# Triangular inverses held as two stacked 64-blocks, in one transformer kernel on a Trainium2 core

## The reference

```
L = where(strict, einsum(kb, k) * decay, 0)
sol = triangular_solve(L, [v * beta, kb * exp(g)], unit_diagonal=True)
S = S * g_last + kd^T v_new ;  o = qd S + a_qk v_new
```

```
sa = state a_t
state = state * w_t + sa b_t^T + v_t k_t^T
y = state r_t
```

## Time and profile before

| | us |
|---|---|
| median of 3 runs (1602.46 to 1609.0) | 1608.83 |
| profiled execution, first to last instruction | 1608.8 |
| TensorE busy | 1542.6 (96%) |
| VectorE busy | 1066.1 (66%) |
| ScalarE busy | 732.4 (46%) |
| GpSimd busy | 69.8 (4%) |

### The profile page before, as it was taken

The page is one execution under the profiler, slowest core; times in us unless marked ns, Lnnn a source line. Parts: engine busy times, 40 slices in busy tenths (PEclk is TensorE's granted clock), DMA queues, the critical chain, the costliest instruction groups (busy, mean ns, idle before and its releaser), DMA issues.

```text
span 1608.8 us, 35749 instructions
## 1 busy us (share of the span) xinstructions
PE 1542.6 (96%) x15477; PEld 1482.4 (92%) x15477; DVE 1066.1 (66%) x1285; ACT 732.4 (46%) x814; POOL 69.8 (4%) x51
## 2 busy tenths in 40 slices
PE   7999999999999999999998999999988899999998
PEld 7999999888999999999988999989876778999997
DVE  5776487764776557664677776466767875777446
ACT  5433346543533444333555434364473444555333
POOL 2000000100100010000101000021000000100000
PEclk9999999998999999999999999999999999999999
DMA  8565545201566555555533665654310012555552
GB/s 272 187 201 189 194 148 183 80 3 54 184 199 192 193 192 181 189 188 183 184 106 110 191 197 188 200 181 158 107 51 3 3 56 80 181 186 194 198 187 76
DMA packets 155064, 243.25 MB, mean 151 GB/s; under 512 B 9283, under 2 KB 106174, under 8 KB 154814
## 3 DMA queue, kind: packets, MB, share of 16 engines
q1 hardware_dynamic: 154510, 240.63, 45.6%
q10 hardware_dynamic: 432, 0.79, 0.2%
HBM read 240.34 MB, written 1.05 MB: 150 GB/s over the span
## 4 chain that ended last, share of the span: by engine, by line
PE 88%; DVE 6%; ACT 3%; issue 1%; DMA 1%; POOL 0%; SPq 0%; ACTq 0%; DVEq 0%
PE dense_ps L2498 25%; PE dense_ps L2499 24%; PE dense_ps L2500 24%; PE dense_ps L450 1%; PE mixer_ps L538 1%; PE mixer_ps L450 1%; DVE w_lo L2868 1%; PE mixer_ps L1756 1%; PE mixer_ps L1183 1%; PE mixer_ps L1174 0%; DVE xT L2986 0%; ACT ly_r L595 0%; DMA raw<-in_ffn_w_gu 0%; ACT score_b L1213 0%; ACT w_hi L2695 0%
## 5 line engine op out<-in xcount | busy, mean ns | idle before, releaser
L2868 DVE TENSOR_TENSOR w_lo<-raw,w_hi 128x2048 fp32r<-128x2048 f32 x225 | 523.0, 2336 | 240.0 <-ACT w_hi L2695 239.2
L2498 PE MATMUL dense_ps<-h_hi,w_hi 128*128 128x256 f32 x2368 | 666.2, 281 | 11.9 <-DVE h_lo L2943 8.3
L2499 PE MATMUL dense_ps<-h_lo,w_hi 128*128 128x256 f32 x2368 | 659.6, 279 | 0.0
L2500 PE MATMUL dense_ps<-h_hi,w_lo 128*128 128x256 f32 x2368 | 659.4, 278 | 0.0
L2695 ACT ACTIVATE w_hi<-raw 128x2048 fp32r<-128x2048 f32 x225 | 428.6, 1914 | 331.2 <-DMA raw<-in_ffn_w_down 115.5
L2498 PEld LDWEIGHTS dense_ps<-h_hi,w_hi 128*128 128x128 f32 x2368 | 449.2, 190 | 18.0 <-issue 17.5
L2499 PEld LDWEIGHTS dense_ps<-h_lo,w_hi 128*128 128x128 f32 x2368 | 447.5, 189 | 0.9 <-issue 0.5
L2500 PEld LDWEIGHTS dense_ps<-h_hi,w_lo 128*128 128x128 f32 x2368 | 447.2, 189 | 0.0
L2498 PE MATMUL dense_ps<-g_hi,w_hi 128*128 128x256 f32 x960 | 265.8, 277 | 0.0
L2499 PE MATMUL dense_ps<-g_lo,w_hi 128*128 128x256 f32 x960 | 265.8, 277 | 0.0
L2500 PE MATMUL dense_ps<-g_hi,w_lo 128*128 128x256 f32 x960 | 265.8, 277 | 0.0
(11 more groups left out here) (554 smaller groups left out, 1781.6 us busy)
## 6 DMA issues: line engine op xcount, KB each, us to landing
raw<-in_ffn_w_gu SPq DMA_DIRECT2D x176, 512.0 KB, 4.7
raw<-in_ffn_w_down SPq DMA_DIRECT2D x88, 512.0 KB, 4.1
raw<-in_w_ff SPq DMA_DIRECT2D x64, 512.0 KB, 4.2
raw<-in_w_in SPq DMA_DIRECT2D x36, 512.0 KB, 4.4
raw<-in_a_w_in SPq DMA_DIRECT2D x32, 512.0 KB, 4.4
raw<-in_a_w_out SPq DMA_DIRECT2D x8, 512.0 KB, 4.1
raw<-in_b_w_in SPq DMA_DIRECT2D x8, 512.0 KB, 4.1
raw<-in_b_w_out SPq DMA_DIRECT2D x8, 512.0 KB, 4.0
```

Source lines behind the costliest of these rows:

```text
L2498: pe.matmul(o, hi, mh, start=start, stop=False)
L2499: pe.matmul(o, hi, ml, start=False, stop=False)
L2500: return pe.matmul(o, lo, mh, start=False, stop=stop)
L2868: dve.tensor_tensor(w_lo[:, p % SLOTS, :], raw[:, p % SLOTS, :], w_hi[:, p % SLOTS, :].bitcast(F32), ALU.subtract).then_inc(lo_ready, 1)
```

## The change

X, XT and y are kept as 128 x 8 x 64: both diagonal blocks of a system lie in the same 64 columns, the first on partitions 0 to 63, the second on 64 to 127. The identity for that form is a new constant, the merge masks are half as wide, and PSUM outputs use columns 0 to 63 on both partition halves. A whole matrix (`inv_w`) is cleared by GpSimd and assembled at the end: after level 5 the diagonal blocks of XT are copied by VectorE in two copies, upper and lower; in the hybrid the systems that need X itself get their diagonal blocks from GpSimd in two copies; level 6 is written straight into it. Where the transposed seed of level 0 comes from SBUF it is merged in two instructions, one for each half. In the hybrid there is one stacked pair for all batches instead of two whole ones; ScalarE resets it after the first solve.

```diff
-                act.activation(y[:, 4 * half:4 * half + 4, :], banks(half, 1), ACT.Copy).then_inc(y_kept, 1)
+                act.activation(y[:, 4 * half:4 * half + 4, :], bank_half(half), ACT.Copy).then_inc(y_kept, 1)
...
+    def bank_half(half, tensor=None):
+        return half_columns(banks(half, 1, tensor))
...
     (inverse_dve)
+                if lv == LEVELS - 1:
+                    dve.tensor_copy(whole_t[UP, h4, LOW], bank_half(half, D_ps)[UP]).then_inc(inv_up, 1)
+                    continue
+                dve.copy_predicated(out=blocks(x[:, h4, :], lv, 0), mask=merge_mask("merge", lv),
+                                    data=blocks(bank_half(half), lv, 0)).then_inc(x_up, 1)
+                if lv:
+                    end_ = dve.copy_predicated(out=blocks(xt[:, h4, :], lv, 1), mask=merge_mask("merge_t", lv),
+                                               data=blocks(bank_half(half, D_ps), lv, 1))
+                else:
+                    for a in (UP, LOW):
+                        end_ = dve.copy_predicated(out=blocks(xt[a, h4, :], lv, 1), mask=merge_mask("merge_t", lv)[a],
+                                                   data=blocks(nt_of(half)[a, :, a], lv, 1))
                 end_.then_inc(inv_up, 1)
+            if lv == LEVELS - 2:
+                dve.wait_ge(inv_up, 14 * batch + 2 * lv + 2)
+                for a in (UP, LOW):
+                    dve.tensor_copy(whole_t[a, :, a], xt[a, :, :])
...
+    def diagonal_pool(pool, parts, batch):
+        pool.wait_ge(x_up, 12 * batch + 2 * (LEVELS - 2) + 2)
+        for k, (to, of) in enumerate(parts):
+            pool.tensor_copy(to, of).then_inc(diag_kept, 1)
+            pool.wait_ge(diag_kept, diag_count(batch + 1) - len(parts) + k + 1)
...
     (inverse4_dve)
+                    for a in (UP, LOW):
+                        dve.copy_predicated(out=blocks(to[a, 0:2], lv, 1), mask=mask_[a, 0:2],
+                                            data=blocks(nt_of(half)[a, :, a], lv, 1))
+                    end_ = dve.copy_predicated(out=blocks(to[:, 2:4], lv, 1), mask=mask_[:, 0:2],
+                                               data=blocks(bank_half(half, D_ps)[:, 2:4], lv, 1))
...
+            if lv == LEVELS - 2:
+                dve.wait_ge(inv_up, 14 * batch + 2 * lv + 2)
+                for a in (UP, LOW):
+                    dve.tensor_copy(by_four(whole, NEED_R[1], a, a), by_four(xt, NEED_R[1], a, UP))
...
     (mixer_a_pool)
+        def begun(g):
+            pool.memset(SET_A[g]["inv_w"][:, :, :], 0.0)
+            pool.tensor_copy(SET_A[g]["inv"][:, :, :], over_mid(constant("ident_half"), 8))
+            pool.tensor_copy(SET_A[g]["inv_t"][:, :, :], over_mid(constant("ident_half"), 8)).then_inc(a_init, 1)
...
     (hybrid: solve, GpSimd, ScalarE, VectorE)
                 if phase == 0:
+                    pe.wait_ge(diag_kept, diag_count(GROUPS_A + i + 1))
...
+        pool.memset(inv_w[:, :, :], 0.0).then_inc(diag_kept, 1)
+        pool.wait_ge(diag_kept, 1)
+        for i in range(RT):
+            diagonal_pool(pool, [(by_four(inv_w[:, :, :], NEED_R[0], a, a), by_four(x_r[:, :, :], NEED_R[0], a, UP))
+                                 for a in (UP, LOW)], GROUPS_A + i)
...
-                if lv == 1 and more and i:
-                    act.wait_ge(r_y, i)
-                    act.activation(X_R[(i + 1) % 2][:, :, :], over_mid(ident, 8), ACT.Copy)
...
+                if phase == 0 and i + 1 < RT:
+                    act.wait_ge(diag_kept, diag_count(GROUPS_A + i + 1))
+                    act.wait_ge(inv_up, 14 * (GROUPS_A + i + 1))
+                    act.activation(x_r[:, :, :], over_mid(constant("ident_half"), 8), ACT.Copy)
+                    act.activation(xt_r[:, :, :], over_mid(constant("ident_half"), 8), ACT.Copy).then_inc(r_init, 1)
...
+            if i == 0:
+                dve.wait_ge(diag_kept, 1)
```

More of the change, by code:

```diff
@@ L438, in blocks, with half_columns, diagonal, stacked @@
         return ap.rearrange("p s (k e b) -> p s k e b", e=2, b=1 << lv)[:, :, :, odd, :]
+    UP, LOW = slice(0, 64), slice(64, P)
     def merge_mask(name, lv):
-        m_ = mask8(name)[:, 64 * lv:64 * lv + 64].rearrange("p (k b) -> p k b", b=1 << lv)
-        return m_.unsqueeze(1).to_broadcast((P, 4, 64 >> lv, 1 << lv))
-    def quads(pe, bank, half, lhs, rhs):
+        m_ = mask8(name)[:, 32 * lv:32 * lv + 32].rearrange("p (k b) -> p k b", b=1 << lv)
+        return m_.unsqueeze(1).to_broadcast((P, 4, 32 >> lv, 1 << lv))
+    def half_columns(ap):
+        return ap[:, :, 0:64]
+    def diagonal(nt_of):
+        return lambda s_, a: nt_of(s_)[a, a]
+    def stacked(x):
+        return lambda s_, a: x[a, s_, :]
+    def quads(pe, to, half, lhs, rhs):
         for s4 in range(4):
[L448 to L451, removed]
-        return end_
-    def inverse_pe(pe, nt_of, x, xt, y, ready, batch, last, beside=lambda lv: None):
-        low, up = slice(64, P), slice(0, 64)
+            for a in (UP, LOW):
+                end_ = pe.matmul(to[a, s4, :], lhs(4 * half + s4, a), rhs(4 * half + s4, a), start=True, stop=True)
+        return end_
+    def bank_half(half, tensor=None):
+        return half_columns(banks(half, 1, tensor))
+    def inverse_pe(pe, nt_of, x, xt, y, ready, batch, beside=lambda lv: None):
+        nt, x_, xt_, y_ = diagonal(nt_of), stacked(x), stacked(xt), stacked(y)
         for lv in range(LEVELS):
@@ L481, in inverse_pe @@
                         s_ = 4 * half + s4
[L482 to L487, removed]
+                        end_ = pe.matmul(to_t[UP, s4, :], y_(s_, LOW), xt_(s_, LOW), start=True, stop=True)
                 end_.then_inc(z_mm, 1)
@@ L585, in inverse4_pe @@
                         s_ = 4 * half + s4
-                        end_ = pe.matmul(D_ps[up, half, P * s4 + 64:P * s4 + P], y[low, s_, up], xt[low, s_, low],
-                                         start=True, stop=True)
+                        end_ = pe.matmul(to_t[UP, s4, :], y_(s_, LOW), xt_(s_, LOW), start=True, stop=True)
                     end_.then_inc(zt_mm, 1)
@@ L596, in inverse4_act, with inverse4_dve @@
             beside(lv)
-    def inverse4_dve(dve, nt_of, x, xt, batch, beside):
+    def inverse4_dve(dve, nt_of, x, xt, whole, batch, beside):
         for lv in range(LEVELS):
             for half in range(2):
+                h4 = slice(4 * half, 4 * half + 4)
                 if lv == 0:
@@ new lines, in inverse4_dve @@
+                turned = 12 * (batch - GROUPS_A) + 2 * (lv - 1) + half + 1
+                if lv == LEVELS - 1:
+                    a, b = (4 * half + at_ for at_ in NEED_R[0])
+                    dve.tensor_copy(whole[LOW, a:b, UP], bank_pair(half)[LOW, NEED_R[0][0]:NEED_R[0][1], :])
+                    dve.wait_ge(zt_mm, turned)
+                    a, b = (4 * half + at_ for at_ in NEED_R[1])
+                    dve.tensor_copy(whole[UP, a:b, LOW],
+                                    bank_half(half, D_ps)[UP, NEED_R[1][0]:NEED_R[1][1], :]).then_inc(inv_up, 1)
+                    continue
```

180 lines of the change are left out of this document (79 added, 101 removed).

## The result

| | before | after |
|---|---|---|
| median of 20 runs (us) | 1609.72 (1601.06 to 1627.04) | 1621.03 (1609.76 to 1631.02) |
| profiled execution, its span (us) | 1608.8 | 1629.1 |

Ratio 1.0058, interval 1.0036 to 1.0081: some 9 us slower, where 5.8 us faster was forecast; the time lies outside the range. (The ratio leaves out runs over 1.5% above a kernel's fastest, so it is smaller than the 11.3 us between the medians.)

A forecast was written before the change was run, and what follows sets the result against it. It took the inverses' ring of TensorE, ScalarE and VectorE taking turns as the bound: hybrid -3.8 and mixer -2.0 gave -5.8 us against 1608.8, so 1603.0 us, range 1596 to 1609.

The forecast's parts named there:

- TensorE's instructions are the same in number and shape: 0: Whole kernel: the change leaves the number and shape of TensorE's instructions alone, so they cost 0 us.
- The signs of being wrong: Inverses: forecast wrong if GpSimd's copies take over 1.2 us or the solve follows ScalarE in all batches.
- The prices: Inverses: ScalarE's copy 0.38 instead of 0.597 us; halved VectorE merges 0.49 instead of 0.78, and 0.29 instead of 0.43.
- (b): Hybrid: GpSimd's two diagonal copies, at 3.10 us each, release the first solve in all four batches; 1612.7 us, chance 0.06.
- (c): Inverses: halved instructions are not cheaper, only assembly counts, +0.5 to 0.7 us in five inverses; 1612 us, chance 0.06.
- the solve released by VectorE: Hybrid batches 0 to 2: assembly copies delay VectorE, leaving gains of 1.27 (batch 0) and 0.96 us instead of 1.75 and 1.49.
- theory V: Follow-up forecast, hybrid: the solve waits for VectorE; with all diagonal copies on GpSimd, batches 0 to 2 get 0.70 us shorter.
- G: Follow-up forecast, hybrid: meeting GpSimd's copies holds VectorE, so four copies there bring no gain or a loss.
- the charge of 0.3 for meeting GpSimd: Hybrid batches 0 to 2: VectorE loses 0.3 us per batch meeting GpSimd's copies, bounds 0 and 0.7.
- rival (a): Inverses: VectorE's end is not binding, switches and GpSimd meeting cost nothing; -10.5 us, some 1598.3 us, chance 0.18.
- The clock at 0: After the mixer's last inverse: gaps before the half-clock stretch get no longer, so TensorE's clock costs 0 us.
- theory C: Follow-up forecast, mixer: 3.4 us at half clock from group 0's first values follow from TensorE's 2.2 us pause.

The follow-up runs named there:

- e4: Kernel before with everything from the squares on 128 bytes lower in SBUF, as in the kernel after: 1626.77 us, ratio 1.0115 to before.
- e1: Kernel before run again unchanged: 1615.05 us, ratio 1.0012 to before.
- e2: Kernel after run again unchanged: 1621.22 us, ratio 1.0076 to before.
- e3: Kernel after with 128 unused bytes behind the masks, so buffers behind them lie at before's addresses: 1606.82 us, ratio 0.9965 to before.
- e14: As e3, with GpSimd making all diagonal copies of the hybrid and those of mixer group 0: 1605.7 us, ratio 0.9933 to before.
- e13: As e3, with GpSimd making all hybrid diagonal copies and 14 filler products on TensorE before group 0's first values: 1607.7 us, ratio 0.9953 to before.
- e17: As e16, with e14's edits added: 1587.87 us, ratio 0.9807 to before.
- e18: Kernel before with w_lo 128 bytes further on and 128 unused bytes behind the masks: 1598.39 us, ratio 0.9873 to before.
- e5 to e12: Eight runs of the kernel after with 32 to 384 unused bytes behind the masks, or every buffer 64 or 128 bytes higher: medians 1603.4 to 1653.3 us.
- e12: Kernel after with 160 unused bytes behind the masks: 1639.9 us, ratio 1.0165 to before.
- e15: Kernel after at before's addresses, but h_lo and g_lo 128 bytes further on than h_hi and g_hi: 1633.2 us, ratio 1.0112 to before.
- e16: Kernel after with h and g at before's addresses, raw and w_lo slots 128 bytes further on, w_hi staying: 1592.0 us, ratio 0.9854 to before.

## Why the prediction was wrong, point by point

The failed step is "TensorE's instructions are the same in number and shape: 0", and with it "the dense stages before and after run on TensorE and are just shifted". The term was +12 to +14 us, not 0 (e4 less e1, e2 less e3; with the -5.2 of the stages below it gives +7 to +9, where +9 was measured): new lengths of two small tensors moved the dense products' operands from distance 192 to 64. The trace of before could have warned of it, though it could not have told what the addresses do: 342 against 355 products in windows that are alike in clock and busy time. The three runs shown before the prediction spread 6.5 us, one stretch's worth. The signs of being wrong that the prediction listed, slow GpSimd copies and a solve that follows ScalarE, both stayed away: they looked at the inverses alone.

**The prices** were right. Rows of after by tile (ns: lowest, median, highest), answering to the earlier trace rows:
```profile
L617 ACT ACTIVATE ly_r<-mixer_ps x48: 366/383/385, 1230.0 to 1345.4; 128x256 f32<-128x256 f32 x48
```
```profile
L638 DVE COPY_PREDICATED x_r<-msk,mixer_ps x48: 292/301/478, 1227.6 to 1344.5; 128x128 f32<-128x128 uint8 x48
```
```profile
L546 POOL COPY inv_w_r<-x_r x8: 391/396/472, 1243.6 to 1345.4; 64x256 f32<-64x256 f32 x8
L656 DVE COPY inv_w_r<-xt_r x8: 285/355/448, 1243.9 to 1345.5; 64x256 f32<-64x256 f32 x8
```
0.38 for ScalarE's copy as said, 0.30 for the merge where 0.29 was said, 0.29 to 0.45 for an assembled copy (0.30 said, bounds 0.23 and 0.43), 0.40 on GpSimd (0.26 said, at most 1.04). Rivals (b) and (c) are out by these rows.

**Hybrid, the solve released by VectorE.** The time line of after, batch 2, answering to the earlier trace rows and to the end of the earlier trace rows:
```profile
1310.36 0.30 DVE L638 COPY_PREDICATED x_r<-msk,mixer_ps 128x128 f32<-128x128 uint8 x1
1310.68 0.30 DVE L643 COPY_PREDICATED xt_r<-msk,dense_ps 128x128 f32<-128x128 uint8 x1
1310.79 0.85 POOL L546 COPY inv_w_r<-x_r 64x256 f32<-64x256 f32 x2 [32.71 <-DVE x_r L638]
1311.02 0.77 DVE L656 COPY inv_w_r<-xt_r 64x256 f32<-64x256 f32 x2
1311.81 0.69 DVE L2218 TENSOR_TENSOR bk<-kk,a_lr 128x512 f32<-128x512 f32 x1
...
1313.24 0.60 ACT L2035 ACTIVATE w_sys<-dense_ps 128x512 f32<-128x512 f32 x1 [1.63 <-PE dense_ps L1807]
...
1314.17 0.28 DVE L635 COPY inv_w_r<-dense_ps 64x128 f32<-64x128 f32 x1
...
1314.60 1.13 PE L1797 MATMUL mixer_ps<-w_sys,inv_w_r 128*128 128x128 f32 x8 [1.39 <-DVE inv_w_r L635]
```
The key products start 1.13 behind the last merge (1.07 said), ScalarE is through at 1313.84, and the solve waits until 1314.60 for VectorE's last copy. From the right-hand side to the solve it is 2.55 us where it was 1.85. In e14, where GpSimd makes all four diagonal copies, the solve follows ScalarE again:
```profile
1290.66 1.20 POOL L549 COPY inv_w_r<-x_r 64x256 f32<-64x256 f32 x2 [30.40 <-DVE x_r L641]
...
1291.92 1.20 POOL L549 COPY inv_w_r<-xt_r 64x256 f32<-64x256 f32 x2
...
1293.34 0.28 DVE L638 COPY inv_w_r<-dense_ps 64x128 f32<-64x128 f32 x1
...
1293.77 1.14 PE L1800 MATMUL mixer_ps<-w_sys,inv_w_r 128*128 128x128 f32 x8 [0.70 <-ACT w_sys L2038]
```
So theory V, not G: 1.86 from right-hand side to solve in e13, e14 and e17, and the charge of 0.3 for meeting GpSimd was too high in after. Where they do meet, both pay: in e14 two copies take GpSimd 1.20 instead of 0.85, and in the mixer a multiplication of 128x1024 beside its copies takes VectorE 1.54 instead of 1.21. The Trainium skill, GPSIMD Engine Reference, section "Specifications", has that as contention with VectorE instructions of two SBUF inputs; the trace agrees.

**The stages in sum.** Group 1's inverse and batch 2 repeat to 0.1 us from profile to profile, whatever the pace, batches 0 and 1 to 0.4. The rest scatters, by some 3 us behind the mixer's inverses, with the clock above all, so the sum is good to about 1 us. The averages are over 4 profiles of the old program (before, e1, e4, e18), 13 of the new one (after, e2, e3, e5 to e12, e15, e16).

| us | forecast | measured | before, after |
|---|---|---|---|
| hybrid batch 0 | -0.87 | -1.2 | 34.75, 33.53 |
| batches 1 and 2 | -0.56 each | -1.0 each | 34.62, 33.61 |
| batch 3 | -1.8 | -0.4 | 31.39, 31.03 |
| mixer to group 0's first values | -0.5 | -1.3 | 35.47, 34.19 |
| from there to product 3080, just ahead of group 1's inverse | 0 | +1.0 | 4.91, 5.86 |
| group 1's inverse | -1.5 | -1.4 | 30.66, 29.22 |
| mixer behind it | 0 | +0.2 | 19.62, 19.82 |
| sum | -5.8 | -5.2 | |

The sum is right partly by luck. Batches 1 and 2 gained more (the last right-hand side came 1.8 earlier, where 1.5 was forecast and 2.0 is rival (a)'s), batch 3 much less. There TensorE stands still before the same product, the 12888th, in all 13 profiles of the new program, for 0.2 to 1.8 us that the trace ascribes to issue; of the old one's four profiles only e4 has a pause near it, of 0.2. All such pauses in the levels of batch 3 come to 1.06 us on average in the new program and to 0.20 in the old: 0.9 of the missing 1.4 us, and the reason why the batch scatters from 30.19 to 31.74. What causes them and where the other 0.5 went stay open.

Of the -1.3 in the mixer's first stage only half is the inverse's. From VectorE's `neg_lt`, behind which the inverse begins, to group 0's first values it is 31.14 us in the old program and 30.55 in the new: -0.6 where -0.5 was forecast. The other 0.7 lies ahead of the inverse. There VectorE makes two splits of weight pieces (`w_lo`) while GpSimd copies identities. In three of the four profiles of the old program GpSimd's second copy is the long one, and the second split takes 3.1 us; in e4, where the first copy was the long one, and in all profiles of the new program it takes 2.3. In the new program GpSimd's copies are half as long, so this may well be a gain of the change, but the forecast had no term for it. The two splits before, then those of after with one of GpSimd's copies beside them:
```profile
302.65 5.46 DVE L2868 TENSOR_TENSOR w_lo<-raw,w_hi 128x2048 fp32r<-128x2048 f32 x2
```
```profile
310.82 4.65 DVE L2915 TENSOR_TENSOR w_lo<-raw,w_hi 128x2048 fp32r<-128x2048 f32 x2
...
314.25 1.70 POOL L996 COPY inv<-cst 128x512 f32<-128x512 f32 x1
```

**The clock at 0.** This was wrong in the mixer. The chip grants the lower level (1.2 GHz) for 3.4 us (6.8 in e12, e15 and e16) about when group 0's first values begin. Rows of the time line of after, then the window behind them, with the columns of the earlier trace rows:
```profile
346.23 0.74 DVE L524 COPY inv_w<-dense_ps 64x256 f32<-64x256 f32 x2
...
347.07 2.05 PE L728 MATMUL mixer_ps<-v_tok,inv_w 128*128 128x128 f32 x8 [2.24 <-DVE inv_w L524]
```
```profile
347.05:351.25 4.20, 4.18 (x24) 4.20 (x25) 2.80 (x3) 4.17 (x3) 0.00 (x0) 0.64 0.03 6
```
The same stretch of before:
```profile
340.30:344.50 4.20, 4.19 (x35) 4.05 (x36) 3.79 (x7) 4.17 (x3) 0.00 (x0) 1.00 0.01 4
```
35 products there, 24 here; the eight first values take 2.05 us instead of 1.13. TensorE's pause ahead of them is 2.24 us here and was 1.15. The dip is in all 13 profiles of the new program and in two of four of the old one (e4, e18): from first values to product 3080 it is 4.20 without it, 5.4 to 6.9 with it. It takes back most of what the stage before it gained. In e13 (pause filled) and e14 (pause 1.57) there is none, which speaks for theory C; but e17, with e14's pause, has it, for 6.8 us (6.73 in that stage). So the pause is not the whole cause: what decides in which executions the clock falls there stays open.

e13 itself missed in the mixer: the fp32 products of the filler went out as 28 instructions, took 3.4 us and made the first values 0.9 later (35.23 after the mixer's start); without the dip the stage behind was 1.6 shorter. e14's came at 33.63 as said (33.5), since VectorE was relieved of 0.86, and the stage behind it took 4.20: matmul 3080 at 37.84, two us before e3's 39.83.

## What to carry to other kernels

A change of a constant's length moves every buffer behind it. Before a result of under 2% is explained by the edit, count the main loop's instructions in equal windows of both traces, and time the old kernel at the new places: here 128 bytes were worth more than the edit, and of the other sign. In a kernel like this one, where TensorE streams one tile of SBUF while the next weights are loaded from another, the addresses of the four kinds of operands modulo 256 bytes are worth a trial of their own: 3% lie between the best and the worst distance here, and some 1% more with `w_lo` apart.

## What the hardware showed unexpectedly

At full clock and with no idle time, products of 128x256 start 113.3, 117.3, 117.8, 118.3, 118.7 or 120.0 ns apart, by the distance of the operands modulo 256 bytes; at distances 192 and 64 a long stretch takes 113.3 or 117.8, for no cause that the traces show, and keeps it. The Trainium skill, TensorE: Matmul & The Clock Gate, section "Wait — 56ns, not 53.3ns?", has a fixed cost of about 2.5 ns per product over its columns at 2.4 GHz; an estimate from that is 109.2 ns for 256 columns, and every pace here is above it. The Trainium skill, SBUF — State Buffer, section "SBUF: two separate sides", says that within the engines' side only the port pair shared by VectorE and GpSimd contends. What the addresses do to TensorE here fits no such pair; where they act inside the chip no run shows. Why `w_lo` moved by 128 bytes ends the draw well, and `h_lo` badly, stays open too, and distance 32 was not tried.
